# A hybrid encoder on one Trainium2 core: wide products in three more places of the sample's group, a norm row by row, a residual add ahead of a head

## The chip, the cores and the metric

The kernel runs on one core of one Trainium2 chip. The metric is the device time of one execution in microseconds (us); three runs of the kernel before took 2398.01 to 2398.31, median 2398.26. The engines are TensorE (PE; PEld is its weight loads), VectorE (DVE), ScalarE (ACT), GpSimd (POOL, idle here) and SyncE (SP, which issues DMAs).

## What is computed

A trunk of two layers runs over two groups of tokens with the same weights: the prompt, P, of 512 tokens, and the sample, S, of 256. Model width is 1024, in 8 tiles of 128 rows. Layer 0 mixes tokens by an S5 state space and a gated linear attention (GLA), layer 1 by differential attention. In each layer a cross attention to 256 memory tokens and an MLP follow:

```
proj = h @ w_in                                   # layer 1: q, k, v of the differential attention
q = rms_norm(q.reshape(..., 8, 2, 64), q_norm) / 8 ; k likewise
...
q = rms_norm((h @ w_q).reshape(..., 4, 256), q_norm) / 16      # cross attention, both layers
x = x + cross_attention(...) ; h = rms_norm(x, norm_mlp)
x = x + square(relu(h @ w1)) @ w2
```

## The kernel before

**Tiles.** Activations lie transposed, model rows on partitions, tokens along the free axis. A product (`Product`, L1199) is cut into output tiles of 128 rows; each takes one weight tile of 1024 x 128 (512 KB). Every fp32 operand is split into a high part that TensorE's fast format holds exactly and a low part, and a tile is high x high, high x low and low x high over 8 blocks of 128. For P that is 24 matmuls of 512 columns, for S 24 of 256 (L1524). The result lies in one of two banks of PSUM, `ps[:, m % 2]`, for the running tile number m.

**Wide tiles.** For S some products, those in the set `WIDE` (L1197), are wide: high and low part of the activations lie side by side, so one matmul of 512 columns gives high x high in the left half of the bank and high x low in the right half (L1510). Then 8 matmuls of 256 columns add low x high (L1512, L1515). Whoever reads the bank must add its two halves: a residual product does so by two adds to x (L1868, L1869), an MLP up product by a reduce on DVE into a ring buffer (L1883), after which ACT works on the ring (L1751 to L1753) and the low part of the hidden values follows one slot later (`dve_up_low`, L1857). The wide ones are seven of the eight MLP products of layer 0, the sample's differential output projection and its cross attention output of layer 0.

**The order of the work.** Python builds a list `slots`; each slot is one tile and a list of steps of other work (norm, cross attention, heads of GLA). All engines walk this list in order, so what an engine does in a slot is written out by hand: TensorE (from L2366) runs the tile, then `pe_post` of the tile before it; ACT (from L2399) splits the high part of the weights three tiles ahead (`high`, L1481), then `act_tile`, then `act_post` of the tile before; DVE (from L2464) makes the low part of the weights two tiles ahead (`low`, L1486), then steps, then `dve_tile`, then `dve_post` of the tile before. Engines wait by semaphores: `td` counts finished tiles, `tf` freed banks. TensorE starts tile m once tile m - 2 has been read out.

**Where the queries stand.** A query tile (kind `q`) is read twice by ACT, squared into a ring (L1729) and copied (L1730, which frees the bank). After each odd tile DVE adds two squares (L1911) and TensorE sums them over the rows (L1538), after the next tile. During the sample's queries of layer 0 the slots also hold the prompt's norm: its root (L1834, L1835), then per row a scaling on DVE (L1929, `dve_apply`), a high part on ACT (L1773) and a low part on DVE (L1936, `dve_fin`). The prompt's queries follow and need those rows. The sample's queries of layer 1 lie among tiles of the prompt's MLP.

**The differential input projection** (kind `qkv`, 24 tiles: 8 q, 8 k, 8 v) of S alternates two tiles with one tile of the prompt's MLP: first an up tile, then eight residual (down) tiles, then three up tiles. For the 16 q and k tiles ACT squares the bank (L1738), copies it (L1741, frees the bank) and takes the high part of the square (L1745); DVE takes the low part (L1876) in the same slot; TensorE multiplies both with a matrix of ones (L1559, L1560) after the next tile; ACT makes the root by a logarithm and an exponential (L1684, L1685) and DVE three operations and a scaling (L1838 to L1840, L1916). A v tile is copied by ACT (L1747), transposed by TensorE (L1566) and copied by DVE (L1919).

**The two other places.** In the first tile of the sample's GLA output projection (`eo`) DVE runs the last head of the prompt's GLA (`dve_finish`, L1834, L1835, L2288 to L2290) and then adds the tile to x (L1869). And the prompt's norm ahead of its layer-1 cross attention runs during ten tiles of the sample's MLP (two up, eight down), in cuts `FINE` = (1, 2, 3, 4, 6, 8), so that the last four rows go in pairs; `ONES` = (1, 2, ..., 8). `added` (L2488) is the rule that puts a sample's residual add ahead of a step's work.

Of the kernel before, what the change touches and what calls it, by code (L numbers as in the profile page):

```python
# [126 lines left out]
def build(nc, params, x_in, mem_in, wt_in, wglu_in, wgate_in, bc_in, tab_in, u_dram, y_dram, k_dram, v_dram, qk_dram, vog_dram,  # L127
          lr_dram, out):
    ctx = ExitStack()
    with ctx:  # L130
# [837 lines left out]
        def trunk_tail(mem, ymem, mem_reload):  # L968
# [225 lines left out]
                    self.out = 64 * XH * layer  # L1194
                    self.first = None

            WIDE = {WT[n] for n in ("dn00", "dn01", "dn02", "dn03", "dout", "o0", "up01", "up02", "up03", )}  # L1197

            class Product:  # L1199


                def __init__(self, kind, g, w0, ready, n=KT, rhs=None, norm=None, up=None, layer=0):
                    z = gs[g]
                    self.kind, self.g, self.w0, self.ready, self.n = kind, g, w0, ready, n
                    self.rhs = (in_h[g], in_l[g]) if rhs is None else rhs
                    self.wide = None
                    if g == "S" and kind in ("res", "up") and w0 in WIDE:
                        if kind == "up":
                            up.low = low_d.take(n)
                        self.wide = hid_w[g] if rhs is not None else in_S[:, :, :, :].rearrange("p z k t -> p k z t")  # L1210
                    self.norm, self.up = norm, up
                    if kind == "q":
                        self.sq, self.qa, self.tq = z["sqd"].take(KT), z["qad"].take(XH), z["tqd"].take(XH)
                        half = XH // 2 * BL[g]
                        self.stats = [Stat(g, None, half, 256, rq[g][:, half * j:half * j + half]) for j in range(2)]
                        for j, s_ in enumerate(self.stats):
                            s_.use, s_.lo = (z["snew"], s_.new), half * j
                    if kind == "qkv":
                        self.sq, self.sl = z["sqd"].take(16), z["sql"].take(16)
                        self.ap = z["ap"].take(16)  # L1220
                        self.stats = [Stat(g, ones64_r[:, :], N[g], 64, y[g]) for _ in range(16)]
                        for i in range(16):
                            self.stats[i].use = (z["ap"], self.ap + i + 1)
                            self.stats[i].bank = 2 if i % 2 == 0 else 6
                        self.vtr, self.vcp = z["vtr"].take(KT), z["vcp"].take(KT)
# [175 lines left out]
            later([("kvload", "P", 1, dP)])  # L1401
            drain()
            run(Product("res", "P", WT["dout"], dP.ready, norm=nP))
            later([], *norm_steps(nP, FINE))
            mS.run(10)
            qp = Product("q", "P", WT["q1"], nP.ready)
            run_q(qp)
# [290 lines left out]
            def act_tile(a, t):  # L1698
# [7 lines left out]
                elif prod.kind == "mem":  # L1706
# [11 lines left out]
                    if i < KT:  # L1718
                        nc.scalar.activation(ring[g][:, j, :], acc_ps, ACT.Square).then_inc(z["sqd"].sem, 1)
                        if prod.layer or h >= 2:  # L1720
                            a.wait_ge(kout[h % 2].sem, prod.layer * 16 * XH + 32 * (h // 2))
                        nc.scalar.activation(ktmp[:, h % 2, j, :], acc_ps, ACT.Copy).then_inc(tf[b].sem, 1)
                    else:
                        nc.scalar.activation(ring[g][:, j, :], acc_ps, ACT.Copy).then_inc(tf[b].sem, 1)
                elif prod.kind == "q":
                    a.wait_ge(td.sem, m + 1)
                    if i >= 2:
                        a.wait_ge(z["tqd"].sem, prod.tq + i // 2)
                    nc.scalar.activation(ring[g][:, i % 2, :], acc_ps, ACT.Square).then_inc(z["sqd"].sem, 1)  # L1729
                    nc.scalar.activation(qx[g][:, i, :], acc_ps, ACT.Copy).then_inc(tf[b].sem, 1)  # L1730
                elif prod.kind == "qkv":
                    a.wait_ge(td.sem, m + 1)
                    if 2 <= i < 18:
# [120 lines left out]
            def dve_up_low(v, t):  # L1854
# [2 lines left out]
                nc.vector.tensor_tensor(hid_l["S"][:, i, :], ring["S"][:, i % 2, :], hid_h["S"][:, i, :].bitcast(F32), ALU.subtract)\  # L1857
                    .then_inc(low_d.sem, 1)

            def dve_tile(v, t):  # L1860
                prod, i, m = t
                g, z, b = prod.g, gs[prod.g], m % 2
                if prod.kind == "res":
                    if prod.w0 == WT["eo"] and i % 4 == 0:
                        v.wait_ge(xl["SP"[i // 4]].sem, 16)
                    v.wait_ge(td.sem, m + 1)
                    if g == "S" and prod.wide is not None:
                        dve_chain(nc.vector.tensor_tensor(x[:, i, cols(g)], ps[:, b, TS:2 * TS], x[:, i, cols(g)], ALU.add))  # L1868
                    nc.vector.tensor_tensor(x[:, i, cols(g)], ps[:, b, 0:N[g]], x[:, i, cols(g)], ALU.add).then_inc(tf[b].sem, 1)  # L1869
                    if prod.norm is not None:  # L1870
                        dve_sum(v, prod.norm, i - 1)
                        if i == KT - 1:
                            dve_sum(v, prod.norm, i)
                elif prod.kind == "qkv" and i < 16:
                    v.wait_ge(z["sqd"].sem, prod.sq + i + 1)
                    nc.vector.tensor_tensor(sq_l[g][:, i % 2, :], ring[g][:, i % 2, :], sq_h[g][:, :].bitcast(F32), ALU.subtract)                        .then_inc(z["sql"].sem, 1)  # L1876
                elif prod.kind == "mem" and i < KT and i % 2 == 1:
                    v.wait_ge(z["sqd"].sem, prod.sq + i + 1)
                    nc.vector.tensor_tensor(ring[g][:, 1, :], ring[g][:, 0, :], ring[g][:, 1, :], ALU.add).then_inc(z["kad"].sem, 1)
                elif prod.kind == "up" and prod.wide is not None:  # L1880
                    v.wait_ge(td.sem, m + 1)
                    both = ring["S"][:, i % 2, :]
                    nc.vector.tensor_reduce(both, ps[:, b, :].rearrange("p (z t) -> p t z", z=2), AX.X, ALU.add).then_inc(tf[b].sem, 1)  # L1883
                elif prod.kind == "up":
                    v.wait_ge(z["hx"].sem, prod.up.hx + i + 1)
                    nc.vector.tensor_tensor(hid_l[g][:, i, :], ps[:, b, 0:N[g]], hid_h[g][:, i, :].bitcast(F32), ALU.subtract)\  # L1886
                        .then_inc(tf[b].sem, 1)
# [447 lines left out]
            with nc.Block() as block:  # L2335
# [129 lines left out]
                def _(v):  # L2465
# [9 lines left out]
                    for n_, (t, steps) in enumerate(slots):  # L2475
# [10 lines left out]
                        if early and not done:  # L2486
                            dve_post(v, before)
                        added = t is not None and t[0].g == "S" and t[0].kind == "res" and t[1] < KT - 1 and any(  # L2488
                            step[0] == "nfin" and step[1].g == "P" for step in steps)
                        for step in steps:  # L2490
                            if step[0] == "cross":
                                dve_cross_max(v, *step[1:])
# [3 lines left out]
                            lows = t[2] + NHI - 1  # L2496
                        if before is not None and before[0].kind == "up" and before[0].wide is not None:
                            dve_up_low(v, before)
                        if added:
                            dve_tile(v, t)  # L2500
                        done = q_first(t, steps)
                        if done:
                            dve_post(v, t)
                        for step in steps:
# [11 lines left out]
                        for step in steps:  # L2516
                            if step[0] == "gla":
                                dve_gla_post(v, *step[1:])
                            elif step[0] == "napply" and ahead:
                                dve_apply(v, *step[1:])  # L2520
                        if t is not None and not added:
                            dve_tile(v, t)
                        if before is not None and not early:
                            if before[0].kind == "mem" and before[1] < KT and before[1] % 2 == 1:
# [120 lines left out]
```

## Time and profile before

| | |
|---|---|
| median of three runs | 2398.26 us (2398.01 to 2398.31) |
| the profiled execution's own time | 2397.84 us |
| its span, first to last instruction | 2396.1 us |
| granted TensorE clock, mean | 1.000 |
| instructions | 34669 |
| a prompt tile (24 matmuls of 512 columns) where nothing waits | 5.44 us from start to start |
| in the projection, two sample tiles and one prompt tile | 11.7 us |
| moved from and to HBM | 267.45 MB, 19.50 MB, 120 GB/s over the span |

The profile is one execution. Its span is 1.7 us shorter than its own time, and that time is 0.42 us below the median. In a row of a timeline the first number is the start in us from the span's start, the second the length; a matmul's length holds its pass through the array, so two that follow each other overlap, and the rate is read from the starts.

### The profile page before, as it was taken

What the parts mean: (1) busy time and instruction counts of PE and PEld (TensorE: products, weight loads), DVE (VectorE), ACT (ScalarE), POOL (GpSimd) and SP (SyncE); (2) the same over time, 40 slices, a digit from 0 to 9 for tenths busy, and PEclk for the clock granted to TensorE, in tenths of its full rate; (3) what the DMA queues carried; (4) which work ended last, traced back from release to release, by engine and by line L of the source; (5) the groups of instructions that cost most, each with busy time, mean ns of one, the idle gap of its engine ahead of it and who ended that gap; (6) DMA issues with size and microseconds to landing.
All of it is one profiled execution on the core that took longest, in us unless ns stands there. A gap on an engine that the chain in (4) does not pass through costs nothing.

```text
span 2396.1 us, 34669 instructions
## 1 busy us (share of the span) xinstructions
PE 2384.5 (100%) x13751; PEld 2019.0 (84%) x13751; DVE 1548.1 (65%) x2626; ACT 1169.3 (49%) x2070; POOL 0.2 (0%) x4
## 2 busy tenths in 40 slices
PE   9999999999999999999999999999999999999999
PEld 6988877888889888998788888888888898888887
DVE  8999668776577876664665448858985565533332
ACT  5334455555435565545453436636764453533432
POOL 0000000000000000000000000000000000000000
PEclk9999999999999999999999999999999999999999
DMA  5445533563224553443234223233234323423322
GB/s 201 106 98 163 211 110 96 171 205 117 69 88 150 193 189 127 134 140 98 79 96 168 88 94 122 93 97 97 91 104 146 118 80 120 126 97 97 97 97 88
DMA packets 109696, 291.30 MB, mean 122 GB/s; under 512 B 18944, under 2 KB 40576, under 8 KB 108256
## 3 DMA queue, kind: packets, MB, share of 16 engines
q1 hardware_dynamic: 100832, 264.83, 34.6%
q10 hardware_dynamic: 8704, 24.25, 3.2%
q8 instruction: 110, 1.80, 0.3%
q14 instruction: 50, 0.41, 0.1%
HBM read 267.45 MB, written 19.50 MB: 120 GB/s over the span
## 4 chain that ended last, share of the span: by engine, by line
PE 86%; DVE 3%; ACT 1%; issue 0%; DVEq 0%; ACTq 0%
PE ps L1524 65%; PE ps L1510 5%; PE ps L1515 3%; PE ps L1638 2%; PE ps L1595 2%; PE ps L1620 2%; PE ps L1662 1%; PE ps L1651 1%; DVE wlo L1486 1%; PE ps L1608 0%; DVE ringP L1929 0%; PE ps L1669 0%; PE ps L2034 0%; PE ps L2101 0%; PE ps L1538 0%
## 5 line engine op out<-in xcount | busy, mean ns | idle before, releaser
L1481 ACT ACTIVATE whi<-wraw 128x1024 fp32r<-128x1024 f32 x430 | 451.9, 1052 | 173.8 <-PE ps L1524 127.2
L1524 PE MATMUL ps<-in_hP,whi 128*128 128x512 f32 x1336 | 533.2, 399 | 1.7 <-DVE in_lP L1936 0.9
L1486 DVE TENSOR_TENSOR wlo<-wraw,whi 128x1024 fp32r<-128x1024 f32 x430 | 522.3, 1217 | 0.2
L1524 PE MATMUL ps<-in_hP,wlo 128*128 128x512 f32 x1336 | 520.9, 390 | 0.0
L1524 PE MATMUL ps<-in_lP,whi 128*128 128x512 f32 x1336 | 520.2, 389 | 0.0
L1524 PE MATMUL ps<-hid_P,whi 128*128 128x512 f32 x1024 | 316.9, 391 | 0.0
L1524 PEld LDWEIGHTS ps<-in_hP,whi 128*128 128x128 f32 x1336 | 250.8, 188 | 60.5 <-issue 5.9
L1524 PEld LDWEIGHTS ps<-in_hP,wlo 128*128 128x128 f32 x1336 | 250.7, 188 | 53.4
L1524 PEld LDWEIGHTS ps<-in_lP,whi 128*128 128x128 f32 x1336 | 251.0, 188 | 51.8 <-issue 1.4
L1524 PE MATMUL ps<-in_S,whi 128*128 128x256 f32 x1536 | 285.4, 287 | 0.5 <-DVE x L1869 0.5
L1869 DVE TENSOR_TENSOR x<-ps,x 128x256 f32<-128x256 f32 (+1 forms) x192 | 106.7, 556 | 261.2 <-PE ps L1524 259.5
L1524 PEld LDWEIGHTS ps<-in_S,whi 128*128 128x128 f32 x1536 | 240.2, 191 | 16.6 <-issue 14.9
L1524 PEld LDWEIGHTS ps<-hid_P,whi 128*128 128x128 f32 x1024 | 190.9, 188 | 41.4 <-issue 2.7
L1524 PE MATMUL ps<-in_S,wlo 128*128 128x256 f32 x768 | 217.2, 283 | 0.0
L1524 PE MATMUL ps<-hid_P,wlo 128*128 128x512 f32 x512 | 199.4, 389 | 0.0
L1886 DVE TENSOR_TENSOR hid_P<-ps,hid_P 128x512 fp32r<-128x512 f32 x64 | 44.3, 692 | 228.7 <-ACT hid_P L1758 228.7
L1756 ACT ACTIVATE ps<-ps 128x512 f32<-128x512 f32 (+1 forms) x104 | 51.9, 500 | 221.5 <-PE ps L1524 221.5
L1524 PEld LDWEIGHTS ps<-in_S,wlo 128*128 128x128 f32 x768 | 147.1, 191 | 0.0
L1524 PEld LDWEIGHTS ps<-hid_P,wlo 128*128 128x128 f32 x512 | 96.1, 188 | 20.2
L1524 PE MATMUL ps<-hid_S,whi 128*128 128x256 f32 x512 | 95.3, 288 | 0.9 <-DVE x L1869 0.9
L1696 ACT ACTIVATE ringP<-x 128x512 f32<-128x512 f32 x40 | 25.3, 633 | 138.9 <-DVE x L1869 122.0
L1524 PEld LDWEIGHTS ps<-hid_S,whi 128*128 128x128 f32 x512 | 79.6, 191 | 14.2 <-issue 13.1
(506 smaller groups left out, 3509.1 us busy)
## 6 DMA issues: line engine op xcount, KB each, us to landing
wraw<-wt SPq DMA_DIRECT2D x432, 512.0 KB, 3.5
wraw<-wt ACTq DMA_DIRECT2D x17, 512.0 KB, 4.1
k_scratch<-region_P SPq DMA_DIRECT2D x16, 256.0 KB, 3.1
v_scratch<-vtmp SPq DMA_DIRECT2D x32, 128.0 KB, 3.6
x<-x_in SPq DMA_DIRECT2D x4, 768.0 KB, 6.7
x<-x_in SPq DMA_DIRECT2D x2, 1536.0 KB, 7.1
mix_mem<-mem_in ACTq DMA_DIRECT2D x1, 2048.0 KB, 15.2
region_S<-k_scratch ACTq DMA_DIRECT2D x2, 1024.0 KB, 7.5
```

Of the source, the lines that this page charges most:

```text
L1481: nc.scalar.activation(whi[:, (n + 3) % NHI, :, :], wraw[:, ws(n), :, :], ACT.Copy).then_inc(wh.sem, 1)
L1486: nc.vector.tensor_tensor(wlo[:, ws(n), :, :], wraw[:, ws(n), :, :], whi[:, (n + 3) % NHI, :, :].bitcast(F32), ALU.subtract).then_inc(wr.s ...
L1510: nc.tensor.matmul(both, w_h[:, k, :], prod.wide[:, k, :, :], start=(k == 0), stop=False)
L1515: last = nc.tensor.matmul(ps[:, m % 2, 0:N["S"]], w_l[:, k, :], h_[:, k, :], start=False, stop=(k == KT - 1))
L1524: last = nc.tensor.matmul(ps[:, m % 2, 0:N[prod.g]], w_[:, k, :], x_[:, k, :], start=(k == 0 and j == 0), stop=(k == KT - 1 and j == 2))
L1595: last = nc.tensor.matmul(ps[:, 3 + q_ % 2, b * 256:(b + 1) * 256], qx[g][:, 2 * h + j, lo:lo + P], km[g][:, 2 * h + j, :], start=(j == 0) ...
L1620: last = nc.tensor.matmul(ps[:, 7, j * 256:(j + 1) * 256], vm[g][:, kt, (2 * h + j) * P:(2 * h + j + 1) * P], at[:, q_ % 2, kt * 256:(kt + ...
L1638: last = nc.tensor.matmul(ps[:, 3 + zz, 0:N[g]], dq[g][rows, h, b * P:(b + 1) * P], dk[g][rows, h, :], start=True, stop=True)
L1696: nc.scalar.activation(ring[nm.g][:, i % 2, :], src, ACT.Square).then_inc(z["sqd"].sem, 1)
L1756: act_chain(nc.scalar.activation(acc_ps, acc_ps, ACT.Relu))
L1869: nc.vector.tensor_tensor(x[:, i, cols(g)], ps[:, b, 0:N[g]], x[:, i, cols(g)], ALU.add).then_inc(tf[b].sem, 1)
L1886: nc.vector.tensor_tensor(hid_l[g][:, i, :], ps[:, b, 0:N[g]], hid_h[g][:, i, :].bitcast(F32), ALU.subtract)\
```

## The change

Three products of the sample join the wide ones: the queries of both cross attentions (`q0`, `q1`, 8 tiles each) and the differential input projection (`din`, 24 tiles). For a query tile DVE now adds the halves by a reduce into the place where ACT's copy went, which frees the bank; ACT squares that. For a q or k tile of the projection the reduce goes to the same place as the copy did, ACT squares it and takes the high part, and DVE takes the low part of the square one slot later (`dve_square_low`), after that slot's weight low part. For a v tile the reduce replaces ACT's copy. In the slot of the layer-0 queries where `q_first` holds, the reduce goes ahead of the norm's step. The prompt's norm ahead of the layer-1 cross attention is cut in single rows, and the `added` rule also holds beside a prompt head's last step.

```diff
-            WIDE = {WT[n] for n in ("dn00", "dn01", "dn02", "dn03", "dout", "o0", "up01", "up02", "up03", )}
+            WIDE = {WT[n] for n in ("dn00", "dn01", "dn02", "dn03", "dout", "o0", "up01", "up02", "up03", "q0", "q1", "din", )}
...
-                    if g == "S" and kind in ("res", "up") and w0 in WIDE:
+                    if g == "S" and kind in ("res", "up", "q", "qkv") and w0 in WIDE:
...
             run(Product("res", "P", WT["dout"], dP.ready, norm=nP))
-            later([], *norm_steps(nP, FINE))
+            later([], *norm_steps(nP, ONES))
...
+                elif prod.kind == "q" and prod.wide is not None:
+                    a.wait_ge(tf[b].sem, m // 2 + 1)
+                    if i >= 2:
+                        a.wait_ge(z["tqd"].sem, prod.tq + i // 2)
+                    nc.scalar.activation(ring[g][:, i % 2, :], qx[g][:, i, :], ACT.Square).then_inc(z["sqd"].sem, 1)
...
+                elif prod.kind == "qkv" and prod.wide is not None:
+                    if i < 16:
+                        a.wait_ge(tf[b].sem, m // 2 + 1)
+                        if i >= 2:
+                            a.wait_ge(z["ssum"].sem, prod.stats[i - 2].sum)
+                        act_chain(nc.scalar.activation(ring[g][:, i % 2, :], (dq, dk)[i // 8][g][:, i % 8, :], ACT.Square))
+                        if i >= 1:
+                            a.wait_ge(z["ssum"].sem, prod.stats[i - 1].sum)
+                        nc.scalar.activation(sq_h[g][:, :], ring[g][:, i % 2, :], ACT.Copy).then_inc(z["sqd"].sem, 1)
...
+            def dve_halves(v, t, to):
+                prod, i, m = t
+                b = m % 2
+                v.wait_ge(td.sem, m + 1)
+                nc.vector.tensor_reduce(to, ps[:, b, :].rearrange("p (z t) -> p t z", z=2), AX.X, ALU.add).then_inc(tf[b].sem, 1)
+
+            def dve_square_low(v, t):
+                prod, i, m = t
+                v.wait_ge(gs["S"]["sqd"].sem, prod.sq + i + 1)
+                nc.vector.tensor_tensor(sq_l["S"][:, i % 2, :], ring["S"][:, i % 2, :], sq_h["S"][:, :].bitcast(F32), ALU.subtract)\
+                    .then_inc(gs["S"]["sql"].sem, 1)
...
+                elif prod.kind == "q" and prod.wide is not None:
+                    dve_halves(v, t, qx[g][:, i, :])
+                elif prod.kind == "qkv" and prod.wide is not None and i < 16:
+                    dve_halves(v, t, (dq, dk)[i // 8][g][:, i % 8, :])
+                elif prod.kind == "qkv" and prod.wide is not None:
+                    if i < 18:
+                        v.wait_ge(z["ssum"].sem, prod.stats[i - 2].sum)
+                    else:
+                        v.wait_ge(z["vtr"].sem, prod.vtr + i - 17)
+                    dve_halves(v, t, ring[g][:, i % 2, :])
...
-                            step[0] == "nfin" and step[1].g == "P" for step in steps)
+                            step[0] == "nfin" and step[1].g == "P" or step[0] == "fin" and step[1].g == "P" for step in steps)
...
+                        if before is not None and before[0].kind == "qkv" and before[0].wide is not None and before[1] < 16:
+                            dve_square_low(v, before)
                         if added:
                             dve_tile(v, t)
                         done = q_first(t, steps)
+                        if done and t[0].wide is not None:
+                            dve_tile(v, t)
                         if done:
                             dve_post(v, t)
...
-                        if t is not None and not added:
+                        if t is not None and not added and not (done and t[0].wide is not None):
                             dve_tile(v, t)
```

## Rows read from the trace of the kernel before

**Rows 1.** The page, first part: busy us, share of the span, instructions.
```profile
PE 2384.5 (100%) x13751; PEld 2019.0 (84%) x13751; DVE 1548.1 (65%) x2626; ACT 1169.3 (49%) x2070; POOL 0.2 (0%) x4
```

**Rows 2.** Waits of PE: waiter, released by, us in total, times, longest.
```profile
PE ps L1524 <- DVE x L1869: 1.4, 2, 0.9
...
PE ps L1559 <- DVE sq_lS L1876: 0.2, 1, 0.2
```

**Rows 3.** Windows: length, busy us (count) per engine, PEclk, DMA share, GB/s.
```profile
746.98:761.38 14.40, 14.40 (x123) 14.40 (x121) 11.87 (x17) 12.33 (x24) 0.00 (x0) 1.00 0.54 181
766.98:783.74 16.76, 16.76 (x98) 14.75 (x97) 15.58 (x25) 8.27 (x9) 0.00 (x0) 1.00 0.60 190
551.07:576.64 25.57, 25.48 (x208) 24.77 (x206) 23.12 (x34) 18.67 (x36) 0.00 (x0) 1.00 0.51 166
1302.03:1326.38 24.35, 24.35 (x205) 24.35 (x204) 11.64 (x15) 12.81 (x24) 0.00 (x0) 1.00 0.54 173
975.96:1045.90 69.94, 69.94 (x456) 64.20 (x455) 51.08 (x85) 38.36 (x77) 0.00 (x0) 1.00 0.42 136
```

**Rows 4.** Groups of instructions, whole run, by form: busy us, mean ns, idle before.
```profile
L1883 DVE TENSOR_REDUCE ringS<-ps 128x256 f32<-128x512 f32 x24 | 16.6, 691 | 7.1 <-PE ps L1515 5.4 <-PE ps L1512 1.6
...
L1751 ACT ACTIVATE ringS<-ringS 128x256 f32<-128x256 f32 x24 | 10.1, 419 | 15.7 <-DVE ringS L1883 15.6
```

**Rows 5.** Timeline of DVE in the layer-0 queries, start and end.
```profile
553.28 2.36 DVE L1486 TENSOR_TENSOR wlo<-wraw,whi 128x1024 fp32r<-128x1024 f32 x2
...
575.44 1.28 DVE L1936 TENSOR_TENSOR in_lP<-ringP,in_hP 128x512 fp32r<-128x512 f32 x2
576.64 1.21 DVE L1486 TENSOR_TENSOR wlo<-wraw,whi 128x1024 fp32r<-128x1024 f32 x1
```

**Rows 6.** Groups of DVE from 557.05 to 579.35 us, two of nine.
```profile
L1936 DVE TENSOR_TENSOR in_lP<-ringP,in_hP 128x512 fp32r<-128x512 f32 x8 | 5.3, 684 | 0.4 <-ACT in_hP L1773 0.4
L1911 DVE TENSOR_TENSOR ringS<-ringS 128x256 f32<-128x256 f32 x4 | 1.7, 421 | 0.2 <-ACT ringS L1729 0.2
```

**Rows 7.** Timeline of ACT at the first query tile of layer 0.
```profile
554.14 0.38 ACT L1729 ACTIVATE ringS<-ps 128x256 f32<-128x256 f32 x1 [0.56 <-PE ps L1524]
...
555.00 0.69 ACT L1684 ACTIVATE yP<-ps,par 128x512 f32<-128x512 f32 x1 [0.20 <-PE ps L1574]
```

**Rows 8.** Timelines of PE and DVE at the first tile of `eo`.
```profile
485.62 0.28 PE L1524 MATMUL ps<-in_S,wlo 128*128 128x256 f32 x1
...
489.70 0.47 PE L1524 MATMUL ps<-in_S,whi 128*128 128x256 f32 x2 [0.49 <-DVE x L1869]
...
485.13 0.70 DVE L1834 SCALAR_TENSOR_TENSOR ps<-ps,region_S 128x512 f32<-128x512 f32 x1 [0.93 <-ACT region_S L1688]
...
489.14 0.42 DVE L1869 TENSOR_TENSOR x<-ps,x 128x256 f32<-128x256 f32 x1
```

**Rows 9.** Timelines of ACT and DVE in the projection, after a residual tile.
```profile
993.54 0.47 ACT L1684 ACTIVATE yS<-ps,par 128x256 f32<-128x256 f32 x1 [3.21 <-PE ps L1560]
...
994.50 0.43 DVE L1838 SCALAR_TENSOR_TENSOR ps<-ps,yS 128x256 f32<-128x256 f32 x1 [0.50 <-ACT yS L1685]
...
996.30 1.22 DVE L1486 TENSOR_TENSOR wlo<-wraw,whi 128x1024 fp32r<-128x1024 f32 x1
```

**Rows 10.** Timeline of ACT in the projection, after the up tile.
```profile
969.48 0.58 ACT L1756 ACTIVATE ps<-ps 128x512 f32<-128x512 f32 x1 [2.98 <-PE ps L1524]
...
971.21 0.47 ACT L1684 ACTIVATE yS<-ps,par 128x256 f32<-128x256 f32 x1
```

**Rows 11.** Groups of DVE in the layer-1 queries, 1302.03 to 1326.38 us.
```profile
L1911 DVE TENSOR_TENSOR ringS<-ringS 128x256 f32<-128x256 f32 x3 | 1.3, 425 | 7.1 <-ACT ringS L1729 7.1
```

**Rows 12.** Timelines of DVE and PE where the layer-1 norm goes in pairs.
```profile
1868.27 0.41 DVE L1869 TENSOR_TENSOR x<-ps,x 128x256 f32<-128x256 f32 x1
...
1872.26 0.41 DVE L1869 TENSOR_TENSOR x<-ps,x 128x256 f32<-128x256 f32 x1
...
1872.82 0.36 PE L1524 MATMUL ps<-hid_S,whi 128*128 128x256 f32 x1 [0.89 <-DVE x L1869]
```

## The prediction

> **What bounds the kernel now.** The page's first part comes first: TensorE is busy for all of the span, VectorE (DVE) for 65%, ScalarE (ACT) for 49% [rows 1]. So the time is the length of TensorE's stream, and a change can act in two ways: it makes the stream shorter, or it makes TensorE wait. The view of TensorE's waits is the second: in the whole run only ten lines of it stand, and the ones that this change can touch are 1.4 us in two waits for a residual add and 0.2 us for a square's low part [rows 2]. There is little to win from waits. But the 65% is a mean, so the third view is by stage [rows 3], in which the reader is to see how full DVE is under each product: in the queries of layer 0 DVE is busy 23.1 of 25.6 us, in the queries of layer 1 only 11.6 of 24.4 us, and in the differential projection 51.1 of 69.9 us. The three wide products meet three different covers.
>
> **The stream.** A narrow tile of the sample is 24 matmuls of 256 columns; a wide one is 8 of 512 and 8 of 256. Five narrow tiles take 14.40 us, 2.88 each; six wide ones take 16.76 us, 2.79 each [rows 3]. So a wide tile gives 0.09 us, and 40 new ones (8 + 8 + 24) give 3.6 us: 0.7 in each query product, 2.2 in the projection. The Trainium skill, page "TensorE: Matmul & The Clock Gate", section "Wait — 56ns, not 53.3ns?", would make it less: a warm matmul costs its columns at 2.4 GHz and about 2.5 ns, so eight fewer matmuls would give only some 0.02 us a tile, 0.8 us in all (an estimate from that page). The windows measure the same two forms of tile in this kernel, so 0.09 stands.
>
> **Queries of layer 0: the price.** Now ACT reads each tile twice out of PSUM (square, copy), and DVE has only four adds there. In the wide form DVE must add the two halves first, by a reduce of 512 to 256 that takes 0.69 us where this kernel already does it [rows 4]; behind it the next operation on DVE starts 0.60 us later, the spacing of 512-column work here (two from 575.44 to 576.64) [rows 5]. Eight of them are 4.8 us on an engine that has no room: from 557.05 to 579.35 DVE runs the prompt's norm (a scaling and a low part for each of 8 rows), the weights' low parts and the adds, and between the norm's root and the end of the product it idles 0.4 and 0.2 us [rows 6]. TensorE's next product starts at 576.64, just as DVE ends the last low parts of the norm [rows 3, 5].
>
> In the new order the reduce of query tile 6 stands behind those last low parts, and the prompt's first query tile needs the bank that it frees. So DVE's queue up to there is the sum. (a) It ends now at 576.64. (b) The norm's root starts later: ACT's logarithm starts at 555.00 after a square and a copy that began at 554.14 [rows 7]; with the wide form DVE is free of a weight low part at 554.41 (553.28 and the 1.13 that such a part occupies [rows 5]), the reduce at 555.10, and the square issues until 555.46, so 0.46 us. (c) The reduces of tiles 1 to 5 go in ahead: 5 x 0.60 = 3.0. (d) At tiles 1, 3 and 5 the add of two squares must wait for reduce, then square: 0.69 + 0.42 and two hand-overs of 0.04, less the 0.60 that the reduce occupies, is 0.59 each, 1.8 in all, in place of 0.18 now; with the rest of the idle time unchanged that adds about 1.4 (the square over SBUF is 0.42 [rows 4]). (e) Then the reduce itself, 0.69, and 0.14 until TensorE moves (as 489.56 to 489.70 in [rows 8]). 576.64 + 0.46 + 3.0 + 1.4 + 0.83 = 582.3. TensorE's own stream, 0.7 shorter, would be there at 575.9, and the stage as it is at 576.64. **So this product costs 5.6 us net**, not a gain. Bounds: 3.0 with (b), (d) and (e) all hidden, and less is excluded since DVE's order is fixed; 6.5 with the last add also in the way. I take the sum, as each term has its row. The debt ends in the prompt's queries, whose tiles take 5.4 us each.
>
> **The differential projection: a longer chain.** Here DVE's total fits: per pair of tiles and one prompt tile it is busy 8.5 of 11.7 us, and two reduces make it 9.7. The order is what counts. Now square and copy start from PSUM 0.2 us after a tile ends, the low part of the square is done in the same slot, and TensorE's product of ones with the squares, sent after the next tile, never waits. In the new code the low part moves to the next slot, behind the reduce, ACT's two passes and one more weight low part. From the end of a prompt tile (zero), with today's durations: the stat product of the odd tile is through at 0.4, ACT's logarithm and exponential at 1.31 (0.47 and 0.42 and their gaps); DVE's three stat operations and scaling take from 1.35 to 3.15 (994.50 to 996.30 [rows 9]); a weight low part 1.13, to 4.28; the even tile's reduce, long due, to 4.97; ACT's square and copy to 5.9 while DVE does the next weight low part to 6.01; the square's low part to 6.43; 0.14 to TensorE. TensorE is there at 0.24 + 2.79 + 2.79 = 5.82, so it **waits 0.75 us** in each of the six pairs that follow a residual tile: 4.5 us. One pair follows an up tile, whose three ACT passes come before the logarithm: 1.72 us from 969.48 to 971.21 where ACT began at once after a residual tile at 993.54, so about 1.5 more [rows 9, 10], a wait of 2.2. The first pair meets a DVE that is less behind: 0.5 by the same steps. The wait of 0.2 that stands there now [rows 2] falls away. V tiles have no squares, and their extra reduce lies in free time. 4.5 + 2.2 + 0.5 - 0.2 - 2.2 (the stream) = **4.8 us slower**. Bounds: -2.2 if the chain were hidden; +18 - 2.2 if every one of the eight pairs waited 2.2.
>
> **Queries of layer 1.** DVE has half of its time free, and idles 7.1 us ahead of three adds [rows 3, 11]. Reduce, square and add end some 1.8 us after a tile, inside the 2.79 of the next. Gain 0.7; at worst nothing.
>
> **x ahead of a head.** At 489.70 TensorE waits for the add of the first tile, which stands behind a head's stat and three products [rows 8]. Ahead of them it waits for its tile until its last matmul ends at 485.9, so the head starts at 486.2 in place of 485.13 and the copy after it 0.2 us later. What follows (the store of v, whose issue the sync queue does ahead of the next weight load, and the second add) is late by that 0.2 and then met again. I take 0.4 of the 0.49 us; bounds 0 and 0.65.
>
> **Norm in single rows.** The pairs make DVE's slot 4.0 us (1868.27 to 1872.26) against TensorE's 2.88; less one scaling and one low part, 0.6 to 0.7 each, a slot with one row is 2.7 [rows 12]. The 0.89 us wait before 1872.82 goes, 1.05 with the restart (that tile's slot is 3.93). The last row comes two tiles later, in the last of the ten MLP tiles, 3 us before the eighth weight block of the query tile needs it. Gain 1.05; bounds 0.5 and 1.1.
>
> **Sum.** +5.6 + 4.8 - 0.7 - 0.4 - 1.05 = +8.25 us. The profiled execution is 2397.84 (span 2396.1), 0.42 below the median of the three runs, 2398.26. I put the sum on the median: 2406.5.
>
> **Rivals.** (1) *The cover holds*: DVE, at 65% and with idle time in the projection, hides the reduces. Then only the stream and the two waits count: 3.6 + 0.4 + 1.05 = 5.05 faster, 2393.2. It decides if TensorE never meets a late bank, that is if DVE idles over 4.8 us in the layer-0 queries; against it are the 0.6 us it idles [rows 6]. 0.06. (2) *Only the first product binds*: weight low parts run far enough ahead to give the 0.75 us back. Then 5.6 - 2.2 - 0.7 - 1.45 = +1.25, 2399.5. For it: DVE's 3 us of idle time in each 11.7 [rows 3]; against: that idle time lies in the wait for tiles, not in the chain. 0.13. (3) *Every pair waits as long as the one after an up tile*: 8 x 2.2 = 17.6 less 2.4, 15.2 in place of 4.8: 2416.9. It needs ACT's three passes ahead of each logarithm, which only one pair has. 0.05. (4) *The clock falls in the stalls*, of up to 3 us in the layer-0 queries: one prompt tile of 5.44 us at 1.2 GHz costs 5.4 more, 2411.9. For it speaks nothing: the granted clock is 1.00, 2.4 GHz, in every stage [rows 3], after waits of up to 0.9 us [rows 2]. 0.04. The Trainium skill's same page, section "HAM oscillation — how this bites in real kernels", says that idle gaps halve the clock; no wait in this trace shows it.
>
> **The numbers.** Forecast 0.72. A measurement of this kernel can tell about 0.2%, 4.8 us, from no change. Faster holds (1) and a little doubt: 0.07. Same holds (2) and forecasts with half the waits (below 2403.1): 0.16. Slower: 0.77. The range takes in both products at two thirds of their price or with the longer bounds: 2401 to 2411.5.
>
> **What would show it.** In the profile after: TensorE's waits list the squares' sum (L1538) and the product with ones (L1559) behind DVE with some 5 and 7 us; the layer-0 queries last about 31 us; DVE there has eight reduces and no idle time beyond waits for ACT; the projection's pairs last 12.3 us in place of 11.7; wide tiles last 2.79; the waits at 489.70 and 1872.82 are gone. I am wrong if DVE idles in the layer-0 queries, or if the product with ones doesn't wait.

## The result, and the profile after

The changed kernel takes 2407.92 us, median of five executions (2407.00 to 2409.05), where the kernel before takes 2398.26 (five, 2398.01 to 2398.42): ratio 1.0040, 95% interval 1.0029 to 1.0050, 9.7 us slower. The forecast was 2406.5 (+8.25), range 2401.0 to 2411.5. The profiled execution is the slowest of the five, 2409.05 (span 2407.2), and its mean granted clock is 0.999. Three of the five have 0.999 (2407.92, 2408.03, 2409.05), two 1.000 (2407.00, 2407.25). That small difference turned out to matter.

The profile page's first part for the changed kernel, answering to [rows 1]: DVE has 25 us more, ACT 9 us less, and TensorE no longer fills its span.

```profile
PE 2386.6 (99%) x13431; PEld 2005.2 (83%) x13431; DVE 1573.0 (65%) x2666; ACT 1159.9 (48%) x2030; POOL 0.2 (0%) x4
```

TensorE's waits in the changed kernel (waiter, released by, us in total, times, longest), answering to [rows 2]:

```profile
PE ps L1559 <- DVE sq_lS L1883: 6.1, 8, 2.1
PE ps L1538 <- DVE ringS L1947: 4.2, 3, 2.6
...
PE ps L1510 <- DVE region_S L1878: 0.3, 1, 0.3
```

The two waits of 1.4 us for a residual add are gone from the list. In their place stand 4.5 us in the layer-0 queries (L1538, L1510) and 6.1 us in the projection (L1559).

The windows of the changed kernel: the layer-0 queries, six pairs of the projection, the layer-1 queries and the last two MLP residual tiles beside the norm in single rows (the first of them is the tile that was held in [rows 12]), answering to [rows 3] and [rows 12]; then 16 us around the longest wait.

```profile
550.99:583.86 32.87, 28.33 (x144) 23.97 (x142) 28.73 (x42) 18.17 (x29) 0.00 (x0) 0.90 0.39 128
985.30:1059.42 74.12, 70.26 (x361) 58.97 (x359) 56.81 (x97) 36.95 (x66) 0.00 (x0) 1.00 0.38 123
1314.92:1338.66 23.74, 23.74 (x141) 20.98 (x140) 16.38 (x22) 11.00 (x17) 0.00 (x0) 1.00 0.52 177
1881.19:1886.95 5.76, 5.76 (x50) 5.76 (x49) 5.76 (x10) 3.16 (x4) 0.00 (x0) 1.00 0.57 187
...
570.00:575.00 5.00, 5.00 (x31) 4.39 (x29) 4.90 (x10) 3.98 (x8) 0.00 (x0) 1.00 0.45 164
575.00:580.00 5.00, 2.43 (x9) 2.02 (x8) 4.52 (x8) 2.09 (x4) 0.00 (x0) 0.73 0.37 116
580.00:584.00 4.00, 4.00 (x15) 3.50 (x14) 3.00 (x5) 1.90 (x3) 0.00 (x0) 0.50 0.01 2
584.00:586.00 2.00, 2.00 (x10) 1.65 (x9) 1.42 (x3) 1.18 (x2) 0.00 (x0) 0.96 0.28 90
```

Against [rows 3] the layer-0 queries grew from 25.57 to 32.87 us (+7.3), the six pairs from 69.94 to 74.12 (+4.2, 0.70 a pair), and the layer-1 queries shrank from 24.35 to 23.74 (-0.6). The two tiles with the norm take 5.76 us, 2.88 each, where the first of them took 3.93 before (1868.89 to 1872.82, the wait included). The third number from the right in the last four lines is the surprise: the granted clock is 0.50, the lower level of 1.2 GHz, from 580 to 584 us.

What happened there is read from the timeline of PE:

```profile
574.06 1.11 PE L1515 MATMUL ps<-in_S,wlo 128*128 128x256 f32 x8
577.74 0.99 PE L1538 MATMUL ps<-par,ringS 128*128 128x1 f32 x4 [2.57 <-DVE ringS L1947]
578.59 3.76 PE L1510 MATMUL ps<-in_S,whi 128*128 128x512 f32 x8
582.15 1.91 PE L1515 MATMUL ps<-in_S,wlo 128*128 128x256 f32 x8
583.86 0.53 PE L1524 MATMUL ps<-in_hP,whi 128*128 128x512 f32 x1
```

and beside it the timeline of DVE:

```profile
576.01 0.69 DVE L1878 TENSOR_REDUCE region_S<-ps 128x256 f32<-128x512 f32 x1
577.17 0.42 DVE L1947 TENSOR_TENSOR ringS<-ringS 128x256 f32<-128x256 f32 x1 [0.48 <-ACT ringS L1729]
577.52 1.41 DVE L1965 SCALAR_TENSOR_TENSOR ringP<-x,par,yP 128x512 f32<-128x512 f32 x2
578.84 1.22 DVE L1486 TENSOR_TENSOR wlo<-wraw,whi 128x1024 fp32r<-128x1024 f32 x1
579.98 1.29 DVE L1972 TENSOR_TENSOR in_lP<-ringP,in_hP 128x512 fp32r<-128x512 f32 x2
581.18 0.69 DVE L1878 TENSOR_REDUCE region_S<-ps 128x256 f32<-128x512 f32 x1
```

DVE's reduce of tile 6 ends at 581.87, so TensorE could have started the prompt's first query tile at 582.0 (the forecast said 582.3). It started at 583.86: behind a wait of 2.57 us query tile 7 took 5.27 us (578.59 to 583.86) in place of 2.79, its matmuls coming at about half the rate. Read so, the stage holds 5.45 us of DVE's queue and 1.85 us of a lower clock.

In the projection the chain is as forecast. DVE behind a residual tile, in the changed kernel, answering to [rows 9]:

```profile
993.97 1.22 DVE L1486 TENSOR_TENSOR wlo<-wraw,whi 128x1024 fp32r<-128x1024 f32 x1
995.11 0.69 DVE L1878 TENSOR_REDUCE region_S<-ps 128x256 f32<-128x512 f32 x1
995.71 1.22 DVE L1486 TENSOR_TENSOR wlo<-wraw,whi 128x1024 fp32r<-128x1024 f32 x1
996.84 0.42 DVE L1883 TENSOR_TENSOR sq_lS<-ringS,sq_hS 128x256 fp32r<-128x256 f32 x1
```

Weight low part, reduce, weight low part, and only then the square's low part that TensorE waits for (0.64 us there; it goes on at 997.40). TensorE at the same place:

```profile
993.81 2.00 PE L1510 MATMUL ps<-in_S,whi 128*128 128x512 f32 x8
995.65 1.11 PE L1515 MATMUL ps<-in_S,wlo 128*128 128x256 f32 x8
997.40 0.36 PE L1559 MATMUL ps<-sq_hS,ones_r 128*128 128x256 f32 x1 [0.64 <-DVE sq_lS L1883]
997.60 0.28 PE L1560 MATMUL ps<-sq_lS,ones_r 128*128 128x256 f32 x1
```

From the tile's start to the product with ones it is 3.59 us, where a wide tile with no wait lasts 2.79. That is 0.80 us for a wait listed as 0.64, because the wait is counted from the end of the last matmul's pass (995.65 + 1.11 = 996.76), while without a wait the next matmul would have started at 996.60.

### The profile page after: what moved, and what is told of

Its sections match the earlier page's. It is cut to its first block, busy times and chain, and to the rows that moved or that the text cites. A ratio compares the mean times of both kernels' runs of the same rounds, so it can differ in the third digit from the quotient of the medians.

```text
span 2407.2 us, 34029 instructions
## 1 busy us (share of the span) xinstructions
PE 2386.6 (99%) x13431; PEld 2005.2 (83%) x13431; DVE 1573.0 (65%) x2666; ACT 1159.9 (48%) x2030; POOL 0.2 (0%) x4
## 4 chain that ended last, share of the span: by engine, by line
PE 84%; DVE 4%; ACT 1%; issue 0%; ACTq 0%
PE ps L1524 62%; PE ps L1510 7%; PE ps L1515 3%; PE ps L1638 2%; PE ps L1595 2%; PE ps L1620 2%; PE ps L1662 1%; DVE wlo L1486 1%; PE ps L1651 1%; PE ps L1608 0%; PE ps L1669 0%; PE ps L2070 0%; PE ps L2137 0%; DVE ringP L1965 0%; PE ps L1538 0%
## 5 line engine op out<-in xcount | busy, mean ns | idle before, releaser
L1510 PE MATMUL ps<-in_S,whi 128*128 128x512 f32 x640 | 171.4, 400 | 0.3 <-DVE region_S L1878 0.3
L1524 PE MATMUL ps<-in_S,whi 128*128 128x256 f32 x896 | 168.3, 289 | 0.0
L1524 PEld LDWEIGHTS ps<-in_S,whi 128*128 128x128 f32 x896 | 140.2, 191 | 15.4 <-issue 13.9
L1510 PEld LDWEIGHTS ps<-in_S,whi 128*128 128x128 f32 x640 | 117.2, 190 | 23.4 <-issue 1.2
L1524 PE MATMUL ps<-in_S,wlo 128*128 128x256 f32 x448 | 126.6, 283 | 0.0
```

The source lines that it names most:

```text
L1510: nc.tensor.matmul(both, w_h[:, k, :], prod.wide[:, k, :, :], start=(k == 0), stop=False)
L1524: last = nc.tensor.matmul(ps[:, m % 2, 0:N[prod.g]], w_[:, k, :], x_[:, k, :], start=(k == 0 and j == 0), stop=(k == KT - 1 and j == 2))
```

## The experiments

Each kernel ran beside the kernel before, whose median was 2398.18 to 2398.21 us each time.

**One part alone.** Three kernels, each with some names of the set `WIDE` and the rules that belong to them.

```diff
-  ... "up03", "q0", "q1", "din", )}
+  ... "up03", "q0", )}                # layer-0 queries alone; FINE, `added` as before
+  ... "up03", "din", )}               # projection alone; FINE, `added` as before
+  ... "up03", "q1", )}                # layer-1 queries, ONES, `added` with "fin"
```

> The kernel before, with the layer-0 sample queries alone made wide. Theory (DVE's queue is the bound of that stage, and the long wait lets TensorE's clock fall): the stage from the first query tile to the prompt's first query tile grows from 25.6 us to 31 to 33 us, three waits for the squares' sum (L1538) with 4 us together, the granted clock below 1.00 behind the longest; time +5.5 us without the fall of the clock, +7.3 with it (2403.8 to 2405.6). Rival (the reduces are hidden, and the loss of the whole change comes from elsewhere): no waits at L1538, clock 1.00, -0.7 us (2397.6).

Measured: 2404.42 us (eight executions, 2403.75 to 2406.47), ratio 1.0027 (1.0017 to 1.0037), +6.2. Its waits and the clock around the longest:

```profile
PE ps L1538 <- DVE ringS L1947: 4.2, 3, 2.6
...
PE ps L1510 <- DVE region_S L1878: 0.3, 1, 0.3
```

```profile
575.00:580.00 5.00, 2.43 (x13) 2.02 (x12) 4.52 (x8) 1.85 (x5) 0.00 (x0) 0.88 0.42 154
580.00:585.00 5.00, 5.00 (x22) 4.17 (x22) 4.51 (x8) 3.27 (x5) 0.00 (x0) 0.78 0.17 34
```

The waits are those of the whole change, to a tenth. The two executions with mean clock 1.000 took 2403.75 and 2403.77, +5.6; the six with 0.999 up to 2406.47. The reduces are not hidden.

> The kernel before, with the differential projection alone made wide. Theory (the square's low part now comes one slot later, behind a reduce, two ACT passes and two weight low parts): the product of ones with the squares (L1559) waits eight times, 2.1 us once and 0.65 in most, 6 us together; each pair of tiles with its prompt tile 12.4 us in place of 11.7; +5.6 us (2403.9). Rival (it is the full DVE of the layer-0 queries that makes this stage late): without the wide queries the waits are gone and only the shorter stream is left, -2.2 us (2396.1).

Measured: 2405.77 us (2403.96 to 2406.01), ratio 1.0031 (1.0019 to 1.0042), +7.6, and so 2 us over the theory. Its waits and two windows:

```profile
PE ps L1559 <- DVE sq_lS L1883: 6.2, 8, 2.1
```

```profile
976.00:980.00 4.00, 1.88 (x9) 1.51 (x8) 3.01 (x5) 2.71 (x6) 0.00 (x0) 0.84 0.51 182
980.00:984.00 4.00, 4.00 (x15) 3.17 (x14) 3.15 (x6) 1.63 (x3) 0.00 (x0) 0.73 0.00 0
```

The waits are there without the wide queries, so the rival falls. The extra 2 us go with the clock again (0.84 and 0.73 in these windows), now behind the projection's longest wait (2.1 us, until 978.55): five of six executions had 0.999, and the one with 1.000 took 2403.96, +5.8, as the theory has it. In the profiled execution of the whole change the same wait of 2.1 us, which ended at 984.99, left the clock alone:

```profile
984.00:988.00 4.00, 3.01 (x14) 2.59 (x15) 2.22 (x5) 3.68 (x7) 0.00 (x0) 1.00 0.38 126
```

> The kernel before, with the other three parts: layer-1 sample queries wide, the norm in single rows, x added ahead of a head. Theory (each of the three meets a DVE with room): -0.7, -1.1 and -0.2 to -0.3, together -2.0 us (2396.2); no wait at L1538 in the layer-1 queries. Rival (their gains in the whole change were only the debts of earlier stages being paid back): no change, within 0.5 us of 2398.3.

Measured: 2396.19 us (2396.00 to 2396.50, eleven executions, mean clock 1.000 in all), ratio 0.9992 (0.9983 to 1.0001); eleven executions below the lowest of before beside them (2397.94). The gain is the 2.0 us expected, not the rival's nothing; the interval of the ratio reaches 1.0001, so it is the separation of the executions that shows it. In the layer-1 queries TensorE has no wait.

**Order or load in the projection.** DVE's slot, changed for tiles of the wide projection:

```diff
+  sides = t is not None and t[0].kind == "qkv" and t[0].wide is not None and t[1] < 16 and t[1] % 2 == 0
+  if sides:
+      dve_tile(v, t)
+  if before is not None and before[0].kind == "qkv" and before[0].wide is not None and before[1] < 16:
+      dve_square_low(v, before)
   if t is not None and lows <= t[2] + NHI - 2 < NT:
       low(v, t[2] + NHI - 2)
...
-  if before is not None and before[0].kind == "qkv" and before[0].wide is not None and before[1] < 16:
-      dve_square_low(v, before)
...
-  if t is not None and not added and not (done and t[0].wide is not None):
+  if t is not None and not added and not sides and not (done and t[0].wide is not None):
       dve_tile(v, t)
```

> The three parts of the run before this one and the wide projection, but with DVE's order in it changed: the reduce of each even tile and the low part of each square stand ahead of that slot's weight low part. Worked out with the durations of the rows: the low part of the even tile's square is through some 0.5 us before TensorE has its two tiles done, so the 0.65 us waits vanish and only the pair behind the up tile still waits, about 1.15 us. Theory (order, not load, was the price): the projection takes 1.2 us less than before, pairs 11.5 us; -2.0 - 1.2 = -3.2 us (2395.0), faster than both kernels. Rival (DVE's load, whatever the order): the waits only move to another place, pairs stay at 12.4 us, +3.6 us (2401.9).

Measured: 2394.99 us (2394.81 to 2395.64), ratio 0.9987 (0.9978 to 0.9996), -3.2. Its wait at L1559, its six pairs, and DVE's new order:

```profile
PE ps L1559 <- DVE sq_lS L1883: 1.0, 1, 1.0
```

```profile
976.51:1045.43 68.92, 68.92 (x360) 59.07 (x359) 56.68 (x97) 37.22 (x66) 0.00 (x0) 1.00 0.40 136
```

```profile
985.21 0.69 DVE L1878 TENSOR_REDUCE region_S<-ps 128x256 f32<-128x512 f32 x1
985.81 1.22 DVE L1486 TENSOR_TENSOR wlo<-wraw,whi 128x1024 fp32r<-128x1024 f32 x1
986.94 0.42 DVE L1883 TENSOR_TENSOR sq_lS<-ringS,sq_hS 128x256 fp32r<-128x256 f32 x1
987.28 1.22 DVE L1486 TENSOR_TENSOR wlo<-wraw,whi 128x1024 fp32r<-128x1024 f32 x1
```

DVE is as busy as in the changed kernel (56.68 against 56.81 us in six pairs), ACT too, yet the pairs take 68.92 in place of 74.12 us and TensorE has no idle time. The same work in another order no longer costs anything: the price in the projection was order, not load.

**The last wait of the projection.** The run above left 1.0 us behind the up tile. Here the up tile moves ahead of the first pair:

```diff
-            mP.run(7)
+            mP.run(8)
...
-                if i % 2 == 1:
+                if i % 2 == 1 and i < 23:
                     mP.run(1)
```

> The best version so far (the wide projection in the changed order of DVE, layer-1 queries wide, norm in single rows, x ahead of a head), with the prompt's eighth up tile ahead of the first pair in place of behind it, so that no up tile, with its three ACT passes, stands between two pairs that need squares; the tiles of the prompt's MLP between pairs all move up by one. Theory (the wait of 1.0 us that is left at L1559 comes from ACT's three passes over the up tile): it vanishes, 1.1 us less with the restart, 2393.9. Rival (it is the start of the projection that is late): the wait stays behind the first or second pair, 2395.0.

Measured: 2393.73 us (2393.44 to 2394.37), ratio 0.9981 (0.9972 to 0.9989), the fastest of all and 4.5 us faster than before. L1559 no longer stands among its waits; the first three that do stand in every run (the first is at the start of the program):

```profile
PE ps L379 <- DVE mix_h L828: 2.5, 1, 2.5
PE ps L1524 <- DVE in_lP L1972: 0.8, 2, 0.6
PE ps L1550 <- DVE vtmp L1944: 0.7, 1, 0.7
```

**Load or order in the layer-0 queries.** First DVE's load is lowered (the prompt's norm, `dve_fin`; the kernel leaves most of that norm's low parts out):

```diff
-  nc.vector.tensor_tensor(in_l[g][:, k, :], ring[g][:, k % 2, :], in_h[g][:, k, :].bitcast(F32), ALU.subtract)
+  w_ = 32 if getattr(nm, "light", False) else N[g]      # light: the prompt's norm ahead of the layer-0 cross attention
+  nc.vector.tensor_tensor(in_l[g][:, k, 0:w_], ring[g][:, k % 2, 0:w_], in_h[g][:, k, 0:w_].bitcast(F32), ALU.subtract)
```

> The layer-0 queries wide as in the run of that part alone, but the low parts of the prompt's norm, which DVE works off in the same stage, are cut from 512 to 32 of their columns (the prompt's low parts of that norm are left out for the other columns, so the queries of the prompt are less exact). Each of the eight takes some 0.1 us in place of 0.60. Theory (DVE's queue up to the reduce of tile 6 sets the stage): 8 x 0.5 = 4 us less queue, so the stage is 27.2 us in place of 31 to 33, the wait at L1538 of 2.6 us falls to 1.3, the clock stays at 1.00, and the time is 2399.8 (+1.6 to +1.9 over before). Rival (the price is the chain reduce, square, add at each odd tile, whatever else DVE has to do): the waits stay and the time stays at 2403.5 to 2404.5.

Measured: 2400.04 us (2399.56 to 2400.51), ratio 1.0007 (0.9998 to 1.0016), +1.8. The stage and its waits (line numbers are one higher in this kernel):

```profile
551.18:578.42 27.24, 25.29 (x143) 21.54 (x142) 23.87 (x42) 16.94 (x28) 0.00 (x0) 1.00 0.49 155
```

```profile
PE ps L1539 <- DVE ringS L1948: 1.9, 2, 1.1
```

4 us less of DVE's work make the stage 4.4 us shorter than in the run of that part alone (31.63 by the same window), a part of it the clock's, which is 1.00 throughout. So DVE's queue sets this stage, as the sum had it. This run alone can't tell load from order, since what it takes out stood ahead of the reduces. Then the order is changed as in the projection:

```diff
-  if done and t[0].wide is not None:
-      dve_tile(v, t)
+  first = t is not None and t[0].kind == "q" and t[0].wide is not None
+  if first:                       # ahead of the steps with dve_fin
+      dve_tile(v, t)
...
-  if t is not None and not added and not (done and t[0].wide is not None):
+  if t is not None and not added and not first:
       dve_tile(v, t)
```

> The layer-0 queries wide as in the run of that part alone, with DVE's order changed in the manner that took the waits out of the projection: each reduce stands ahead of that slot's low parts of the prompt's norm in place of behind them. Theory (here it is load, not order: from the norm's root on DVE has no idle time that an order could use): the reduce of tile 6 ends some 2.3 us sooner, since two low parts and a weight low part fall behind it, but the wait at L1538 stays above 2 us; the prompt's first query tile starts 3.1 us later than before in place of 5.5; 2401.4 with the clock at 1.00, up to 2403 where it falls. Rival (order is all, as in the projection): the waits vanish and the stream's gain is left, -0.7 us (2397.6).

Measured: 2402.95 us (2401.49 to 2404.77, eleven executions), ratio 1.0020 (1.0011 to 1.0029), +4.7; the three executions with mean clock 1.000 took 2401.49, 2401.62 and 2402.43. The waits, the clock, and the end of tile 6 on TensorE with its reduce on DVE:

```profile
PE ps L1538 <- DVE ringS L1947: 3.6, 3, 2.0
```

```profile
575.00:580.00 5.00, 3.08 (x12) 2.58 (x13) 5.00 (x9) 2.76 (x5) 0.00 (x0) 0.82 0.36 110
580.00:585.00 5.00, 5.00 (x23) 4.33 (x23) 4.34 (x6) 2.60 (x4) 0.00 (x0) 0.84 0.28 105
```

```profile
573.82 1.11 PE L1515 MATMUL ps<-in_S,wlo 128*128 128x256 f32 x8
579.16 0.68 DVE L1878 TENSOR_REDUCE region_S<-ps 128x256 f32<-128x512 f32 x1
```

This order gives 2.3 us back (2403.76 to 2401.5, both at clock 1.000) and 3.3 us stay, as expected of a full DVE: from 575 to 580 it is busy for all 5.00 us. So order was part of the price here too. That the remaining 3.3 us are load is argued and not shown: the reduce of tile 6 still starts 4.2 us after its tile's end (574.93 to 579.16), behind low parts, an add, two scalings and a weight low part. An order that puts it ahead of those as well was not tried.

**The clock.** Matmuls whose result nobody uses are sent ahead of the longest wait, so that TensorE works in it:

```diff
+  if prod.wide is not None and h == 2:          # in the projection: i == 2, 14 matmuls, ahead of the wait at L1559
+      for _ in range(16):
+          nc.tensor.matmul(ps[:, 2, 256:512], ones64_r[:, :], in_h["S"][:, 0, :], start=True, stop=True)
   pe.wait_ge(z["qad"].sem, prod.qa + h + 1)
```

> The layer-0 queries wide as in the run of that part alone, with 16 matmuls more, 256 columns each, into unused columns of the statistics bank, sent ahead of the third wait at L1538, the one of 2.6 us: about 1.9 us of work that fills the wait (it computes nothing that is used). Theory (the spread of that run, 2403.75 to 2406.5, is the granted clock, which falls when TensorE stands in that wait): the clock is 1.00 through the stage and 1.000 in the mean of every run, all runs within 0.6 us of 2403.8. Rival (the spread has nothing to do with the wait): the same spread, median 2404.4 or above.

> The wide projection as in the run of that part alone, with 14 such matmuls ahead of the one wait at L1559 that lasts 2.1 us (the pair around the up tile): some 1.7 us of work that computes nothing that is used. In that run five of six executions had a mean clock of 0.999 and took 2405.4 to 2406.0, one had 1.000 and took 2403.96; its windows show 0.84 and 0.73 in the 8 us behind this wait. Theory (the clock falls in this wait and costs 1.8 us): clock 1.000 in all runs, median 2403.9. Rival (the clock falls for another reason, or over all eight waits): median stays at 2405.8, or falls by less than 0.5.

Measured: the queries 2403.66 us (2403.30 to 2404.62, eleven executions), ratio 1.0022 (1.0013 to 1.0031); the projection 2403.65 us (2403.51 to 2405.07, nine), ratio 1.0023 (1.0014 to 1.0033). All twenty executions have a mean clock of 1.000, where eleven of fourteen had 0.999 without the matmuls. The windows behind the two waits, first the queries, then the projection:

```profile
575.00:580.00 5.00, 4.42 (x33) 4.07 (x32) 4.52 (x8) 1.89 (x3) 0.00 (x0) 1.00 0.58 197
580.00:585.00 5.00, 4.17 (x22) 3.45 (x21) 4.71 (x7) 3.25 (x6) 0.00 (x0) 1.00 0.27 93
```

```profile
976.00:980.00 4.00, 3.68 (x24) 3.18 (x24) 2.52 (x4) 3.17 (x7) 0.00 (x0) 1.00 0.45 139
980.00:984.00 4.00, 4.00 (x20) 3.21 (x19) 3.26 (x7) 1.18 (x2) 0.00 (x0) 1.00 0.00 0
```

TensorE had 16 and 14 matmuls more to do, and yet the medians are 0.8 and 2.1 us below those of the runs without them. Most of that is what the fall of the clock in these waits had cost: the executions without the matmuls that kept a mean clock of 1.000 lie 0.7 (2403.76) and 1.8 us (2403.96) below their medians. Not all of the spread is the clock: one execution of the queries lay 0.8 above 2403.8, and two of the projection near 2405, at clock 1.000; executions of before at that clock, run beside them, reached 2399.6.

## Why the prediction was right, and where it was off

- **The sign and the sum.** Right. By the profiled execution: +7.3 (layer-0 queries), +5.6 (projection, from its first tile to its end), -0.6, -0.3, -1.1, and 0.2 that stand before 250 us, where nothing was changed: +11.1, and the spans differ by 11.1 (2407.2 less 2396.1). Without the 1.85 us of the clock and the 0.2 the parts make +9.05, and the two executions with clock 1.000 lie 8.7 and 9.0 over before. That the forecast of 8.25 came so close is in part luck, by the next two points.
- **Queries of layer 0.** Forecast 5.6; 5.45 by the trace, 5.6 by the run of that part alone with the clock up. The steps hold: DVE's queue ran to 582.0 (forecast 582.3), and three adds each waited 0.48 us for ACT (forecast 0.59). The run with lighter low parts shows that the sum was over the right thing. One figure in it was a slip: by its own words step (d) adds 1.8 less 0.18, 1.6 and not 1.4, which would have made the product 5.9. The trace has 1.3 (three times 0.48, less 0.18), so the slip happened to help. What the sum took as given is that DVE's order is fixed: another order gave 2.3 us back.
- **Differential projection.** Forecast 4.8, measured 5.6 in the whole change and, alone with the clock up, 5.8 (5.5 with the matmuls in its longest wait). The chain and its places were right: eight waits, 0.17, 2.10 and six of 0.65 (forecast 0.5, 2.2, 0.75). The term that was mis-sized is the price of a wait: the sum took the wait itself, but a tile with a wait of 0.65 lasts 3.60 us in place of 2.79, and the product with ones behind it 0.07 more, 0.88 in all. That restart of 0.23 is 1.8 us over eight waits. The waits themselves were forecast 1.0 us too long (7.2 in all, 6.2 measured), and the two errors leave the missing 0.8. For the norm of [rows 12] the restart had been counted.
- **Layer-1 queries, x ahead of a head, norm.** Forecast -0.7, -0.4, -1.05; measured -0.6, -0.3, -1.1, and -2.0 together in a run of their own. The add now runs when its tile ends (DVE at 486.22, TensorE's next tile at 489.25 in place of 489.70), but some of it is met again in the two tiles after, 3.06 and 2.94 us long.
- **What failed** is the step of rival (4) that begins "For it speaks nothing". It concluded from a clock of 1.00 after waits of up to 0.9 us, while the same sentence put the new stalls at up to 3 us. The rival got 0.04; three of the five executions show the lower mean clock that goes with it, at a smaller price than the 5.4 us put on it: the tile hit was a sample's and lost 2.5 us in the profiled execution, 1.85 of them behind the end of DVE's queue. The Trainium skill, page "TensorE: Matmul & The Clock Gate", section "HAM oscillation — how this bites in real kernels", says that idle gaps, DMA waits in its example, bring TensorE back to half its clock; the trace agrees on the half, with 0.50 behind the wait of 2.57 us, here a wait for DVE and shorter than the gaps of that example.
- **Rivals (1) to (3).** That the cover holds, and that only the first product binds, are refuted by the waits at L1538 and L1559; that every pair waits 2.2 is refuted by the six waits of 0.65.

## What to carry to other kernels

Before an engine gets more work, ask of each place separately whether it lacks time or only stands in the wrong order: in the projection the same work in another order went from 5.6 us lost to 1.2 won, and in the layer-0 queries, where DVE is nearly full, the one other order tried gave back 2.3 of 5.6 us. A share of 65% busy tells neither. Where a change makes TensorE wait, count with each wait the restart behind it, 0.2 us here, and for a wait of 2 us and more the chance of a lower clock, some 2 us more here; behind waits of up to 1.1 us the mean clock stayed at 1.000.

## What the runs showed of the hardware

The granted clock fell from 1.00 to 0.50 behind single waits of TensorE of 2.0 to 2.6 us, and was 1.00 again within 7 us in the four profiled executions that show it. Executions with a mean of 0.999 took 0.1 to 3.3 us longer than the fastest of the same kernel at 1.000; not all of that need be the clock, since executions at 1.000 also differ, by up to 1.6 us (2403.51 to 2405.07). It is not certain to fall: behind the wait of 2.1 us it did in five of six executions of the projection alone and not in the profiled one of the whole change, behind the 2.0 us of the reordered queries in eight of eleven. The mean stayed at 1.000 in every execution where the longest of these waits was 1.1 us (the lighter low parts, eleven executions) or 1.0 (the projection in its new order, eleven). The wait of 2.5 us at L379 in every list says nothing on this: it stands ahead of the program's first matmul. A mean to three places would not show a fall shorter than some 2.4 us (an estimate: 0.0005 of 2400 us, twice, as the clock halves). What decides behind the waits of 2.0 to 2.6 us is open; it wasn't tried. Matmuls without use, 14 to 16 of them in the wait, kept the mean clock at 1.000 in all twenty executions and cost nothing that can be measured.
